# Scores between halves of a block in a chunkwise scan: only the other half's queries are streamed, both directions fill one bank, and all matmuls come after the projection unit

## What is computed

```python
b = jnp.cumsum(lf, axis=2)
rel = b[:, :, :, None] - b[:, :, None, :]
decay = jnp.where(mask, jnp.exp(jnp.minimum(rel, 0.0)), 0.0)
attn = jnp.einsum('bnthk,bnshk,bntshk->bnhts', qc, kc, decay)
o_intra = jnp.einsum('bnhts,bnshv->bnthv', attn, vc)
```

## Time and profile before

| what | value |
|---|---|
| median of 3 runs | 1704.35 us |
| span of the profiled execution | 1699.0 us |
| mean granted clock of TensorE | 0.988 |
| TensorE matmuls (PE) | 1639.3 us, 96% |
| TensorE weight loads (PEld, beside PE) | 1375.0 us, 81% |
| VectorE (DVE) | 971.8 us, 57% |
| ScalarE (ACT) | 671.0 us, 39% |
| DMA | 195.05 MB, mean 115 GB/s |

### The profile page before, as it was taken

The page is one execution under the profiler, slowest core; times in us unless marked ns, Lnnn a source line. Parts: engine busy times, 40 slices in busy tenths (PEclk is TensorE's granted clock), DMA queues, the critical chain, the costliest instruction groups (busy, mean ns, idle before and its releaser), DMA issues.

```text
span 1699.0 us, 30283 instructions
## 1 busy us (share of the span) xinstructions
PE 1639.3 (96%) x12956; PEld 1375.0 (81%) x12956; DVE 971.8 (57%) x1366; ACT 671.0 (39%) x978; POOL 0.2 (0%) x4
## 2 busy tenths in 40 slices
PE   7999999999989998998999999999999999999997
PEld 5787787788778876776788888888878888888886
DVE  7514635755555556667886666666575444444437
ACT  4433337433923481255764454454431221022103
POOL 0000000000000000000000000000000000000000
PEclk7999999999999999999999999999999999999999
DMA  9541323232433337231322232222471222022103
GB/s 368 193 172 54 105 84 127 83 108 83 150 104 101 100 112 276 63 109 53 149 97 84 99 111 74 99 105 98 164 277 50 112 112 95 16 111 111 56 1 124
DMA packets 64381, 195.05 MB, mean 115 GB/s; under 512 B 8593, under 2 KB 18833, under 8 KB 64017
## 3 DMA queue, kind: packets, MB, share of 16 engines
q1 hardware_dynamic: 61536, 182.73, 30.2%
q10 hardware_dynamic: 2736, 10.73, 1.6%
HBM read 137.85 MB, written 55.58 MB: 114 GB/s over the span
## 4 chain that ended last, share of the span: by engine, by line
PE 50%; DVE 1%; DMA 1%; ACT 0%; issue 0%; SPq 0%; DVEq 0%
PE bank L96 16%; PE bank L97 16%; PE bank L98 16%; DMA hid_raw<-hidden 0%; PE bank L1311 0%; DVE hid_lo L1120 0%; PE bank L753 0%; DMA hidden<-c 0%; DVE x L1382 0%; DVE y_tok L1410 0%; DVE down_lo L1126 0%; SPq L1096 0%; DVE c L932 0%; DVE c L934 0%; PE bank L866 0%
## 5 line engine op out<-in xcount | busy, mean ns | idle before, releaser
L96 PE MATMUL bank<-hid_hi,down_lo 128*128 128x512 f32 (+1 forms) x768 | 273.3, 356 | 3.1 <-DVE x L1382 1.5
L97 PE MATMUL bank<-hid_lo,down_hi 128*128 128x512 f32 (+1 forms) x768 | 272.4, 355 | 0.0
L98 PE MATMUL bank<-hid_hi,down_hi 128*128 128x512 f32 (+1 forms) x768 | 271.6, 354 | 0.0
L1382 DVE SCALAR_TENSOR_TENSOR x<-bank,mod,x 128x512 f32<-128x512 f32 (+1 forms) x216 | 142.2, 661 | 222.4 <-PE bank L98 222.3
L96 PE MATMUL bank<-h_lat_hi,in_lo 128*128 128x512 f32 x512 | 208.6, 407 | 5.0 <-DVE h_lat_lo L402 5.0
L98 PE MATMUL bank<-h_lat_hi,in_hi 128*128 128x512 f32 x512 | 200.6, 392 | 0.0
L97 PE MATMUL bank<-h_lat_lo,in_hi 128*128 128x512 f32 x512 | 200.3, 391 | 0.0
L96 PEld LDWEIGHTS bank<-hid_hi,down_lo 128*128 128x128 f32 x768 | 145.2, 189 | 25.6 <-DVE x L1382 2.7
L98 PEld LDWEIGHTS bank<-hid_hi,down_hi 128*128 128x128 f32 x768 | 145.0, 189 | 20.4
L97 PEld LDWEIGHTS bank<-hid_lo,down_hi 128*128 128x128 f32 x768 | 145.3, 189 | 19.9
L1109 ACT ACTIVATE hid_hi<-hid_raw 128x1280 fp32r<-128x1280 f32 x32 | 40.7, 1274 | 297.6 <-DMA hid_raw<-hidden 297.6
(11 more groups left out here) (265 smaller groups left out, 3295.9 us busy)
## 6 DMA issues: line engine op xcount, KB each, us to landing
hid_raw<-hidden SPq DMA_DIRECT2D x32, 640.0 KB, 7.2
in_raw<-in_w_in SPq DMA_DIRECT2D x32, 512.0 KB, 6.7
mx_ada_raw<-in_w_ada_rest SPq DMA_DIRECT2D x32, 512.0 KB, 4.7
up_raw<-in_w_ff SPq DMA_DIRECT2D x32, 512.0 KB, 4.2
hidden<-c SPq DMA_DIRECT2D x64, 256.0 KB, 2.0
down_raw<-in_w_ff SPq DMA_DIRECT2D x32, 512.0 KB, 7.2
proj<-mx_stage ACTq DMA_DIRECT2D x16, 640.0 KB, 6.1
x<-x_scratch SPq DMA_DIRECT2D x16, 640.0 KB, 5.8
```

The source lines that it names most:

```text
L96: nc.tensor.matmul(out, w_lo, x_hi, start=start, stop=False)
L97: nc.tensor.matmul(out, w_hi, x_lo, start=False, stop=False)
L98: return nc.tensor.matmul(out, w_hi, x_hi, start=False, stop=stop)
L1382: nc.vector.scalar_tensor_tensor(xs, self.unit_bank(u)[:, 0:tn], g.m(40 + m, int(b > 0)), xs, ALU.mult, ALU.add).then_inc(self.unit_added[ ...
```

## The change

Both directions of a level are computed in one go behind the unit, into one bank. For each row block and direction the 32 keys are loaded as before, but only the 16 queries of the half that this direction uses are streamed (every second one at level 0, pairs at level 1 and so on, by an access pattern with a gap), and the 16 result columns are written at those queries' own places in the square. As direction 0 fills the right halves and direction 1 the left ones, the two interleave to a full square, and one mask (wanted where key half and query half differ) and one masked copy serve both; the masks shrink from 11 to 6. `level_scores` waits once for both directions' products (`QK_N` and `qk_count` count half as many increments). The middle of the unit is free of other work.

On VectorE the rows of q, f and k lie in one tensor `qfk` in an order in which one access pattern reaches both directions (`in_rows`; q0 and q1 swap places). A level is one multiplication of the keys and one of the queries, of 1280 elements each, one folding of the totals and one masked copy, instead of four, two and two instructions.

The core of the diff (left out: the same renaming at other waits, and the removed `half` argument of `turns`):

```diff
--- before.py
+++ after.py
@@ -53,7 +53,7 @@
 NVEC = _at
 LEVELS = 7
 MASKED = 5
-MASKS = 1 + DIRS * MASKED
+MASKS = 1 + MASKED
 POS_COLS = 4 * (LAT // GRID_W) + 4 * GRID_W
 
 KB = 1024
@@ -518,10 +518,9 @@
     def __init__(self, sem):
         uses = [("diag",)]
         for l in range(MASKED):
-            uses += [("level", l, 0)]
             if l + S_LEVELS == S_TURN:
                 uses += [("vt", n) for n in range(3)]
-            uses += [("level", l, 1)]
+            uses += [("level", l)]
         uses += [("half32",), ("half64", 0), ("half64", 1)]
         uses += [("kt", d, n) for d, n in STATE_ORDER] + [("ds", d, n) for d, n in STATE_ORDER]
         uses += [("out", n) for n in range(3)] + [("sum", n) for n in range(3)]
@@ -1480,10 +1479,16 @@
         ada_raw = buf("ada_raw", [P, 2, D_MODEL], 114)
 
         at_row = lambda i: 122 + 5 * i
-        q = [buf("q0", row, at_row(0)), buf("q1", row, at_row(2))]
-
-        f = [buf("f0", row, at_row(1)), buf("f1", row, at_row(3))]
-        k = [buf("k0", row, at_row(4)), buf("k1", row, at_row(5))]
+        qfk = buf("qfk", [P, 6, TOKENS], at_row(0))
+        ROW_Q1, ROW_F0, ROW_Q0, ROW_F1, ROW_K0, ROW_K1 = range(6)
+        q = [qfk[:, ROW_Q0, :], qfk[:, ROW_Q1, :]]
+        f = [qfk[:, ROW_F0, :], qfk[:, ROW_F1, :]]
+        k = [qfk[:, ROW_K0, :], qfk[:, ROW_K1, :]]
+
+        def in_rows(row, column, *dims):
+
+            return bass.AP(qfk, row * TOKENS + column, [[6 * TOKENS, P]] + [list(d) for d in dims])
+
         v = buf("v", row, at_row(6))
         scores = buf("scores", [P, CHUNKS, P], at_row(6))
         gate = buf("gate", row, at_row(7))
@@ -1561,17 +1566,14 @@
 
             eng.wait_ge(staged[t % 2], (h * (PER_HEAD // 2) + t // 2) * 3 + 3)
 
-        def qk_count(level, d):
-
-            return 1 + d if level == 0 else 2 + (2 * (level - 1) + d) * 2 + 2
-
-        def turns(eng, project, mix, out, half=None):
+        def qk_count(level):
+
+            return 2 + DIRS * level
+
+        def turns(eng, project, mix, out):
 
             def with_step(h, u, last, h_mix, step):
-                if half is None:
-                    project(h, u, last)
-                else:
-                    project(h, u, last, lambda: half(h_mix, step))
+                project(h, u, last)
                 mix(h_mix, step)
 
             def turn(h, last):
@@ -1955,14 +1955,10 @@
                     elif not first(i):
                         pe.wait_ge(staged[1], (i - 1) * 3 + b + 2)
                     for kt in range(KT):
-                        if kt == KT // 2:
-                            between()
                         ins = exact_product(nc, g.bank[u % 2][:, 0:(CTX + 2, 512, 512)[b]], ring.hi[:, s, kt * P:(kt + 1) * P],
                                             ring.lo[:, s, kt * P:(kt + 1) * P], norm.moving(g.h_hi, kt, b),
                                             norm.moving(g.h_lo, kt, b), kt == 0, kt == KT - 1)
                     ins.then_inc(used[s] if b == 2 else unit_full[b], 1)
-                else:
-                    between()
                 if u == 0 and not first(h):
                     turn_rows(h - 1)
                 if b == 2 and not (first(h) and j == 0):
@@ -1981,15 +1977,6 @@
                     last = nc.tensor.transpose(g.bank[2][:, REST + b * P:REST + (b + 1) * P],
                                                g.mod_rows[:, b * P:(b + 1) * P], g.ident[:, :])
                 last.then_inc(rows_turned, 1)
-
-            def square_scores(h, name):
-
-                d = name[2]
-                for c in range(CHUNKS):
-                    for j in range(4):
-                        ins = nc.tensor.matmul(g.bank[bk.bank(name)][32 * j:32 * j + 32, c * 32:(c + 1) * 32],
-                                               blocks(k[d], c, 32, j), blocks(q[d], c, 32, j), start=True, stop=True)
-                bk.filled(ins, name)
 
             def transpose(h, name, src, c0, kc):
                 bk.wait_free(pe, h, name)
@@ -1998,15 +1985,18 @@
                                               src[:, (c0 + c) * P:(c0 + c + 1) * P], g.ident[:, :])
                 bk.filled(ins, name)
 
-            def level_scores(h, level, d):
-                name = ("level", level, d)
+            def level_scores(h, level):
+                name, size = ("level", level), 2 ** level
                 bk.wait_free(pe, h, name)
-                pe.wait_ge(qk_ready, h * QK_N + qk_count(level, d))
-                square_scores(h, name)
-
-            def half_mix(h, step):
-                if S_LEVELS <= step < S_LEVELS + MASKED:
-                    level_scores(h, step - S_LEVELS, 0)
+                pe.wait_ge(qk_ready, h * QK_N + qk_count(level))
+                parts = lambda t, at_block: t[:, at_block:at_block + 32].rearrange("p (n two s) -> p n two s", two=2, s=size)
+                for c in range(CHUNKS):
+                    for j in range(4):
+                        for d in range(DIRS):
+                            out = parts(g.bank[bk.bank(name)][32 * j:32 * j + 32, :], c * 32)[:, :, 1 - d, :]
+                            ins = nc.tensor.matmul(out, blocks(k[d], c, 32, j), parts(q[d], c * P + 32 * j)[:, :, 1 - d, :],
+                                                   start=True, stop=True)
+                bk.filled(ins, name)
 
             def mix(h, step):
                 if step == S_TURN:
@@ -2025,11 +2015,11 @@
                                     blocks(k[d], c, 32, j), blocks(q[d], c, 32, j), start=(d == 0), stop=(d == 1))
                     bk.filled(ins, ("diag",))
                 if S_LEVELS <= step < S_LEVELS + MASKED:
-                    level_scores(h, step - S_LEVELS, 1)
+                    level_scores(h, step - S_LEVELS)
                 if step == S_HALF32:
 
                     bk.wait_free(pe, h, ("half32",))
-                    pe.wait_ge(qk_ready, h * QK_N + qk_count(MASKED, 1))
+                    pe.wait_ge(qk_ready, h * QK_N + qk_count(MASKED))
                     for c in range(CHUNKS):
                         for j in range(4):
                             d = j % 2
@@ -2159,27 +2149,27 @@
 
                 size = 2 ** level
                 pairs = TOKENS // (2 * size)
-                for d in range(DIRS):
-                    for name in ([("level", level, d)], [("half32",)], [("half64", 0), ("half64", 1)]
-                                 )[max(0, level - MASKED + 1)]:
-                        bk.wait_full(dve, h, name)
-                    totals = f[d][:, :].rearrange("p (n two s) -> p n two s", two=2, s=size)
-                    if level:
-                        dve.wait_ge(tot_ready, h * 14 + 2 * (level - 1) + d + 1)
-                    for t, half in ((q[d], 1 - d), (k[d], d)):
-                        part = t[:, :].rearrange("p (n two b) -> p n two b", two=2, b=size)[:, :, half, :]
-                        nc.vector.tensor_tensor(part, part, totals[:, :, 1 - half, 0:1].broadcast_to([P, pairs, size]),
-                                                ALU.mult).then_inc(qk_ready, 1)
-                    dve.wait_ge(qk_ready, h * QK_N + qk_count(level + 1, d))
-                    if level < MASKED:
-                        bk.wait_read(dve, h, ("level", level, 0) if d else ("level", level - 1, 1) if level else ("diag",))
-                    nc.vector.tensor_tensor(totals[:, :, 0, 0], totals[:, :, 0, 0], totals[:, :, 1, 0], ALU.mult
-                                            ).then_inc(tot_ready, 1)
-                    if level < MASKED:
-                        name, mask = ("level", level, d), 1 + 2 * level + d
-                        bk.read(nc.vector.copy_predicated(
-                            diag[:, :, :], masks[:, mask:mask + 1, :].bitcast(I32).broadcast_to([P, CHUNKS, 32]),
-                            g.bank[bk.bank(name)][:, 0:CHUNKS * 32].rearrange("p (c t) -> p c t", t=32)), name)
+                for name in ([("level", level)], [("half32",)], [("half64", 0), ("half64", 1)])[max(0, level - MASKED + 1)]:
+                    bk.wait_full(dve, h, name)
+                if level:
+                    dve.wait_ge(tot_ready, h * LEVELS + level)
+                half = [(2 * size, pairs), (1, size)]
+                keys = in_rows(ROW_K0, 0, ((ROW_K1 - ROW_K0) * TOKENS + size, 2), *half)
+                queries = in_rows(ROW_Q1, 0, ((ROW_Q0 - ROW_Q1) * TOKENS + size, 2), *half)
+                spread = [(2 * size, pairs), (0, size)]
+                key_totals = in_rows(ROW_F0, size, ((ROW_F1 - ROW_F0) * TOKENS - size, 2), *spread)
+                query_totals = in_rows(ROW_F1, size, ((ROW_F0 - ROW_F1) * TOKENS - size, 2), *spread)
+                nc.vector.tensor_tensor(keys, keys, key_totals, ALU.mult).then_inc(qk_ready, 1)
+                nc.vector.tensor_tensor(queries, queries, query_totals, ALU.mult).then_inc(qk_ready, 1)
+                dve.wait_ge(qk_ready, h * QK_N + qk_count(level + 1))
```

(16 more changed lines are left out.)

8 lines of the change are left out of this document (4 added, 4 removed).

## The result

The changed kernel takes 1713.9 us (median of 20 runs) where the kernel before takes 1704.1: a ratio of **1.0052, 95% interval 1.0038 to 1.0066**. So it is slower by 9 to 10 us, inside the range, and just over the half per cent for which the prediction had 0.22 (against 0.61 for a smaller change); the sum had said +2.4. The profiled execution of after took 1714.05 us, next to its median, with a span of 1712.1.

The account below looks back on a forecast made before the run. The prediction took TensorE's own queue, matmuls busy for 96% of the span, as the bound; -3.2, 0, -1.9, +7.5 and 0 summed to +2.4 us, added to the median 1704.35 and rounded down: 1706 us, range 1692 to 1719.

Parts of the forecast that it names:

- One run in place of two sets, -3.2: Level scores on TensorE: running both directions together saves 0.18 us a level in 18 levels, -3.2 us, at most -5.4.
- Sixteen queries, 0: Level score matmuls: halving the streamed columns saves 0 us, as each load stays at 32 columns; far end -11.6.
- VectorE, -1.9: TensorE's waits for VectorE's multiplications before level and 64-wide scores shrink: -1.9 us, bounds -4 and +1.
- The stalls, +7.5: Merged level runs outpace the 256-instruction blocks: seven places, five at 2.0 us, two at 4.5; +7.5 us, bounds -8 and +25.
- The clock, 0: Clock drops behind long stalls in the last head: as many as before, three, so 0 us, bounds -5 and +7.
- The base: Whole kernel: the change is added to the runs' median, 1704.35 us, which lies 5.35 us above the span of 1699.0.
- A: Level scores: the stream sets the pace, -11.6 us, of which stalls take 3 back, 1697 us; chance 0.12.
- D: Block fetches cost no more than now, only the terms -3.2 and -1.9 are left, 1699 us; chance 0.03.
- B: Levels: block fetch becomes the bound, a 1.7 us stall in each of 18 new runs, +21, 1725 us; chance 0.15.
- C: Instruction blocks meet free queues: shorter stalls and no clock drops, -13 on the forecast, 1693 us; chance 0.10.

Follow-up runs that it names:

- e5: The change with one loop turned round: within a chunk the four row blocks of direction 0, then those of direction 1; ratio 1.0062.
- e1: The change, but each score matmul streams all 32 queries and writes the full 32 x 32 square; 1713.2 us, ratio 1.0053.
- e6: e5 with each matmul loading only 16 keys and filling 16 partitions, so half of the scores are wrong or left out; ratio 1.0047.
- e2: The kernel before with direction 0's set moved from mid unit to right ahead of direction 1's, behind the unit; 1712.7 us, ratio 1.0047.
- e4: The change with 128 more TensorE instructions (32 one-element matmuls) at the program's start; ratio 1.0027.
- e7: The change with 64 keys loaded per matmul, half as many instructions, loops turned as in e5, part of the scores left out; 1683.9 us, ratio 0.9890.
- e9: The change with squares of 64 for diag and levels, 64 keys per matmul, two banks and two masked copies, everything computed; 1686.4 us, ratio 0.9903.
- e11: e9 with TensorE waiting behind each of the 20 levels for the first of VectorE's two products; 1735.0 us, ratio 1.0178.
- e12: e9 with TensorE waiting behind each of the 20 levels for both of VectorE's products; 1783.5 us, ratio 1.0463.
- e8: The kernel before with 192 more TensorE instructions (48 one-element matmuls) at the program's start; 1700.1 us, ratio 0.9984.
- e10: The change with each level's matmuls in two runs, the first at depth 7 of the unit, one direction's row blocks after each other; 1705.1 us, ratio 1.0017.

## Why the prediction was right, and by how much not

The time is inside a wide range, and the sign of the sum is right. The size is not: of the 14.4 us that the stretch grew by in the profiled pair the sum had 2.4, and most of the difference is one term, the clock.

**One run in place of two sets, -3.2.** Right. A level is 1.66 and 0.20 us, 1.86 in place of 2.08: 18 x -0.22 = -4.0. The diag order that I took is the slow one; e5 would have shown 1.67 with the edges.

**Sixteen queries, 0.** The number is right (e1: 1 us), the reason is not. I read from the line with one streamed column that the load sets the pace. With 32 columns that does not hold: halving the load too saved 0.04 us (e6), and what is left is a time for each instruction. The gapped access patterns cost nothing that shows. The Trainium skill (TensorEngine Tiling (Array Packing), Instruction Overhead) has a matmul of one streamed column take as long as one of 60, by which the term would be 0 as well; the trace agrees but for 0.06 us a level.

**VectorE, -1.9.** Waits before level and 64-wide scores went from 3.8 us to 0.4, so -3.4. I had feared 0.1 to 0.6 us at diag and in the last head; they didn't come. Busy time fell by 16.8 us, not by 27: multiplications (-8.6) and copies (-10.3) are as forecast, but folding 640 totals takes 1310 ns where 320 took 761, so this loses 5 us and not 9; and of the 24 us that the records lose, 7 had lain beside each other. None of it reached the end. With the first term the work is 7.7 us less, where the sum had 5.1.

**The stalls, +7.5.** By the groups that I had summed to 22.3, after has 31.1 + 1.4 + 1.1 = 33.6: +11.3. That the stalls lie on the grid of 256 and come with runs of many instructions is what e2, e4, e7 and e9 show from four sides. The mechanism is right in the main, the places and prices are not. Of seven places named, head 0's levels 1 (2.0 us) and 3 (6.8), head 2's level 0 (3.5), head 3's levels 0 (6.4) and 2 (2.0) stalled; head 2's levels 2 and 4 did not. That makes 20.8 us where I had 19, which is luck: of the two places priced at 4.5 one cost 6.8 and the other 2.0, and one priced at 2.0 cost 6.4. Head 2's level 2 holds one boundary in the trace, not two. Its level 4 holds both and still ran through, so a whole block inside a run need not stall, and why it did not is open:

```profile
523.57 1.73 PE L1997 MATMUL bank<-mx_qfk 128*32 128x16 f32 x160
525.22 0.50 PE L96 MATMUL bank<-h_lat_hi,in_lo 128*128 128x512 f32 x1
```

The excess came from bursts with a single boundary, which I had at 0.2 to 2 us each: level 3 of heads 1, 2 and 3 stalled for 3.2, 3.4 and 4.6 us. There the packet started 5.2, 5.4 and 7.5 us after the block was entered; head 1's level 3:

```profile
345.00 0.70 PE L1997 MATMUL bank<-mx_qfk 128*32 128x16 f32 x49
348.73 1.74 PE L1997 MATMUL bank<-mx_qfk 128*32 128x16 f32 x111 [3.03 <-issue]
```

The two bursts of 6.4 and 6.8 are two stalls each, as two blocks in a row came late. The Trainium skill's rule that is cited with this term (Runtime: NRT & Kernel Launch, Instruction fetch mechanics), that crossing a block is mostly hidden, would have made it 0; the traces differ: 38.4 us of stalls in e2, 0.8 in e9.

**The clock, 0. This is the step that failed.** Bounds were -5 and +7; it is +11.0 in the profiled pair, of which 3.4 may be put to the quick execution of before. That leaves 7.6, still past the bound. The median clock says the same: 0.986 to 0.980 is 0.006 x 1714 = 10 us lost at half clock at most. I had read three drops behind stalls of over 3 us and took that for a threshold, and counted the stalls that would pass it as before. The trace of before already spoke against it: the idle time of 3.20 us to 186.89 has no drop behind it.

```profile
186.89:193.70 6.81, 6.81 (x109) 5.28 (x108) 5.42 (x12) 0.00 (x0) 0.00 (x0) 1.00 0.23 65
```

e11 shows drops behind idle times of 1.65 us, half as long, and e12 shows one behind every idle time of 3. In the stretch after has seven stretches at half clock, five of 6.8 us and two of 3.4, before three of 3.4. So a threshold of 3 us misprices stalls; a rate does better, but it is not a constant: 0.19 us of clock to a microsecond of stalls in before, 0.31 in e8, 0.44 in after, 0.55 in e10; beyond their waits e11 and e12 grew by 0.45 and 0.54 us for each microsecond waited. At 0.44 the 25.2 + 7.5 us of stalls in my sum lose 14, 10 more than before's 4.8, and +2.4 becomes +12, a little above what the medians show. This rate is read from after itself, so it explains the size and could not have foretold it; at before's 0.19 the sum would be +4.

**The base.** I took the 5.35 us between span and median as time around the span; it is 1.95, and 3.4 were the luck of that execution. The forecast went by the median, so this did no harm there, but it does to any reading of two single profiles.

**Rivals.** A is out by e1, D by the stalls, which rose by 11.1 us. B had a stall in each burst, +23 us; 11 of 20 levels are clean and it is +11. It counted two more clock drops, +3, where the forecast had none and +11 came; with its +21 it overshot the medians' 9.8 by more than the forecast fell short. C, free queues, did not happen: the loads are there. One slip in the chances: the 0.17 for faster takes the forecast's 0.03 whole, where the 0.22 for slower takes its 0.12 as a share of 0.60; taken alike it is 0.15.

## What to carry to other kernels

On an engine whose instructions come in blocks, count instructions per microsecond, not only busy time: 320 short ones in a row use a block up in 1.2 us, often ahead of the next one's arrival, and half as many, each with twice the area and half of it for nothing, made the kernel 27 us faster than the change. "Issue" as the releaser in the middle of a run, on a grid of 256, is the sign. And an idle microsecond of TensorE costs up to one and a half here, since the clock behind it falls, so a merge which gathers small pieces into one run has to be priced with the idle time that it makes.

## What the hardware showed that I had not expected

- With the row blocks taking turns, 160 records of narrow matmuls took 1.56, 1.47 and 1.43 us for 32 x 32, 32 x 16 and 16 x 16 columns loaded and streamed, 4.9 to 4.5 ns an instruction: almost nothing for half the width.
- Two matmuls behind each other in the same row block cost more than with the four taking turns: 1.66 against 1.47 us for 160 records.
- The clock fell behind idle times of 1.65 us in half of the cases (e11), for 3.4 us each.
- The packet of a block came up to 7.5 us after the block before it was entered, in one case when a load of 1 MB on another queue had ended, 2.6 us after the block was needed; from the packet to the next matmul it took 2.2 to 2.8 us in every stall of after.
- What isn't settled: why the clock falls behind one idle time of 1.65 us and not behind the next, why some stretches at half clock last 6.8 or 10.2 us and others 3.4, and why head 2's level 4 runs through two boundaries. No run here separates the load's share from the grid's in the long stalls either, since no load was moved: a packet starts late mostly where the queues are full, but at 675.20 it started early although they were.
